# Branch C's local attention ahead of its states, branch D's token shift on GpSimd, and 12 instead of 14 early gate tiles

## The chip, the core and the metric

One core of a Trainium2 chip runs one program. The time is that of the device in microseconds. The engines are TensorE (PE; its weight loads are PEld), VectorE (DVE), ScalarE (ACT), GpSimd (POOL) and SyncE (SP, which only issues transfers here). They run side by side and wait for one another on semaphores. SBUF is the memory on the core, PSUM the eight banks that TensorE writes.

## The reference, cut to what matters

Three blocks follow one another on 512 tokens of width 1024. Only the first is touched. It projects the tokens, runs four mixers A to D on slices of the projection, and merges them under gates:

```
ys = jnp.stack([ya, yb, yc, yd], axis=2)
gates = jax.nn.sigmoid(p["gate"].reshape(bsz, seq, N_BRANCHES, D_MODEL))
merged = jnp.sum(gates * jnp.einsum('bsnc,ncd->bsnd', ys, w_branch[l]), axis=2)
x = _layer_norm(DN_ALPHA * x + merged @ w_out[l], ln_g[l, 0], ln_b[l, 0])
```

Branch C works in chunks of 64 tokens. Its output is a masked product inside each chunk plus the product with the state before the chunk, and the state is a chain over the chunks:

```
att = jnp.where(causal, jnp.einsum('bnihd,bnjhd->bnhij', q_dec, k_inv), 0.0)
o_intra = jnp.einsum('bnhij,bnjhv->bnihv', att, vc)
def step(state, inp):
    d, u = inp
    return d[..., None] * state + u, state
o = o_intra + jnp.einsum('bnihd,bnhdv->bnihv', q_dec, before)
```

Branch D first mixes each token with the one before it, then goes through a long recurrence:

```
def _token_shift(z, mu):
    prev = jnp.pad(z, ((0, 0), (1, 0), (0, 0)))[:, :-1]
    return z + (prev - z) * mu
```

After the first block come a mixture of experts with 32 experts and two more layers, neither of which the change edits.

## The kernel before, in words

Activations lie feature-major: a tile is 128 features by 512 tokens in fp32, and `pj` holds the 21 projected tiles. The program is a row of stages. Each `stage` ends with a barrier of all engines, and inside it every engine has its own list of instructions in the order in which the code writes them. There is no planner: the order is the code's. Where a step of DVE reads what the step before wrote, `Order` adds a semaphore wait.

The first block's stages in order are the projection, the attention of branches A and B in one stage (`attention`, called by `mixers_ab`), two small products, branch C (`mixer_c`: decays, a transposition, chunks and states, then `head_norm`), branch D (`mixer_d`: token shift, low-rank products, exponents, a transposition, `delta_chunks`), and `merge`.

The weights of the projections are split into a high and a low half, and a product is three matmuls (lines 193 to 195). `merge` computes 32 gate tiles (8 blocks of 3 matmuls each) and 32 branch tiles (2 blocks of 3), multiplies and adds them. Weights come in chunks of 16 blocks, which ACT rounds (line 160) and POOL or DVE subtracts (line 167).

Some of the 32 gate tiles are computed earlier, one fp32 matmul per block (line 251), as filler between the small matmuls of the mixers. `EARLY_GATES` says which. `k.gates.fill(pe, n)` puts n blocks into TensorE's list, `copy` lets ACT bring a finished tile to SBUF (line 262), and `move` lets SP store it to memory and load the next weights. In `merge` ACT loads these tiles back (line 680) and takes their sigmoid.

Before, 112 blocks (14 tiles) are filled in: 32 in the attention, 16 in branch C's decays, 8 in `head_norm`, and 16, 16 and 24 in the first three stages of `mixer_d`. Branch D's token shift is a stage by itself: 21 DVE instructions (lines 1497 to 1499), 16 filler blocks on TensorE, a table load on ACT.

In the attention, a step handles two units. TensorE computes scores (L881), DVE adds the bias and finds the maximum (L983, from a PSUM bank and an SBUF strip for branch A), ACT takes the exponential (L937), DVE divides in SBUF (L989 and L990), TensorE transposes the result (L896), ACT copies it (L946) and TensorE multiplies it with the values (L910). POOL has nothing to do there.

In branch C's stage of chunks TensorE computes the state updates (L1399), the scores within the chunks (L1405), and then for each half of the output the product with the states (L1412) and the product inside the chunks (L1417) into one bank. DVE makes the states (L1430, L1431), then masks the scores (L1437), and copies the result (L1441).

## Time and profile before

| | us |
|---|---|
| median of 3 runs (lowest, highest) | 2757.49 (2756.34, 2758.59) |
| the profiled execution's own time | 2755.97 |
| its span from the first to the last instruction | 2754.2 |
| PE busy in the span | 2615.7 (95%) |
| DVE busy | 1072.6 (39%) |
| ACT busy | 779.2 (28%) |
| POOL busy | 887.9 (32%) |

How to read it: the span lies 1.8 us inside the profiled execution's time. An engine's busy time is the time with at least one of its instructions under way. A row of the timeline gives start, duration, engine, line, operation, output and inputs, and in brackets the idle time before it with what ended it. A row of the windows gives a stretch, its length, the busy time and the number of instructions of PE, PEld, DVE, ACT and POOL, then the granted clock of TensorE (1.00 is 2.4 GHz, 0.50 is 1.2 GHz), the busy share of the DMA engines and GB/s. An fp32 matmul appears as two records.

### The profile page before, as it was taken

How to read it: one execution, taken by the hardware profiler on the slowest of the kernel's cores; microseconds unless marked ns; L12 is line 12 of the kernel's file. 1: busy time of each engine (PE TensorE's matmuls, PEld its weight loads, DVE VectorE, ACT ScalarE, POOL GpSimd, SP SyncE). 2: the span in 40 equal slices, each digit the busy share in tenths (PEclk: the TensorE clock that was granted, in tenths of full speed). 3: DMA queues.
4: the chain of work that ended last, by engine and by line, in shares of the span. 5: the costliest groups of instructions: out<-in, count | busy, mean ns of one | idle time of the engine just before them, and what ended most of it. 6: DMA issues, size and time to landing. Idle time of an engine off the chain costs nothing. (4 is left out here: it accounts for less than half of the span.)

```text
span 2754.2 us, 30647 instructions
## 1 busy us (share of the span) xinstructions
PE 2615.7 (95%) x12344; PEld 1917.8 (70%) x12344; DVE 1072.6 (39%) x1785; ACT 779.2 (28%) x1117; POOL 887.9 (32%) x273
## 2 busy tenths in 40 slices
PE   8988789999889999899999999999999999999998
PEld 6764448788533335784888888888675888888886
DVE  4854345355231113367344411222276444411211
ACT  3023222332121112526322422322326222422311
POOL 4620000044123332230444444444320444444443
PEclk9999789899989999999999999999999999999999
DMA  4431110133469996222222222222240222222223
GB/s 166 155 120 60 46 65 1 46 115 107 199 245 389 392 391 264 86 101 27 92 94 106 92 92 97 102 92 103 104 105 15 95 95 104 92 92 98 101 92 122
DMA packets 84173, 341.56 MB, mean 124 GB/s; under 512 B 34390, under 2 KB 34774, under 8 KB 48448
## 3 DMA queue, kind: packets, MB, share of 16 engines
q1 hardware_dynamic: 64216, 316.28, 31.6%
q10 hardware_dynamic: 5992, 14.87, 1.6%
q0 software_dynamic: 13824, 8.44, 1.0%
q8 instruction: 99, 1.62, 0.2%
q14 instruction: 42, 0.34, 0.0%
HBM read 381.04 MB, written 29.79 MB: 149 GB/s over the span
## 5 line engine op out<-in xcount | busy, mean ns | idle before, releaser
L167 POOL TENSOR_TENSOR w_lo<-w_raw,w_hi 128x2048 fp32r<-128x2048 f32 x148 | 689.2, 4656 | 1541.2 <-ACT w_hi L160 1520.4
L193 PE MATMUL bank<-xh,w_hi 128*128 128x512 f32 x1752 | 697.3, 398 | 29.5 <-DVE w_lo L373 10.9
L194 PE MATMUL bank<-xl,w_hi 128*128 128x512 f32 x1752 | 687.0, 392 | 0.0
L195 PE MATMUL bank<-xh,w_lo 128*128 128x512 f32 x1752 | 686.8, 392 | 0.0
L193 PEld LDWEIGHTS bank<-xh,w_hi 128*128 128x128 f32 x1752 | 332.2, 190 | 112.9 <-issue 30.2
L160 ACT ACTIVATE w_hi<-w_raw 128x2048 fp32r<-128x2048 f32 x150 | 286.4, 1909 | 360.5 <-PE bank L193 338.7
L194 PEld LDWEIGHTS bank<-xl,w_hi 128*128 128x128 f32 x1752 | 332.0, 189 | 73.2 <-issue 5.0
L195 PEld LDWEIGHTS bank<-xh,w_lo 128*128 128x128 f32 x1752 | 331.9, 189 | 69.3
L193 PE MATMUL bank<-ha,w_hi 128*128 128x512 f32 x480 | 186.7, 389 | 0.0
L194 PE MATMUL bank<-hb,w_hi 128*128 128x512 f32 x480 | 186.7, 389 | 0.0
L195 PE MATMUL bank<-ha,w_lo 128*128 128x512 f32 x480 | 186.7, 389 | 0.0
L2992 DVE TENSOR_TENSOR yb<-bank,mats 128x512 f32<-128x512 f32 x64 | 44.3, 692 | 205.8 <-PE bank L195 205.8
L251 PE MATMUL bank<-res,w_raw 128*128 128x512 f32 x224 | 110.7, 649 | 1.9 <-PEq L293 1.9
L3028 DVE TENSOR_TENSOR yb<-yb,bank 128x512 f32<-128x512 f32 x44 | 30.2, 687 | 203.3 <-PE bank L195 203.3
L2958 ACT ACTIVATE yb<-yb 128x512 f32<-128x512 f32 x64 | 40.4, 632 | 241.4 <-DVE yb L2992 241.4
L193 PEld LDWEIGHTS bank<-ha,w_hi 128*128 128x128 f32 x480 | 90.1, 188 | 18.8
L195 PEld LDWEIGHTS bank<-ha,w_lo 128*128 128x128 f32 x480 | 90.1, 188 | 18.7
L194 PEld LDWEIGHTS bank<-hb,w_hi 128*128 128x128 f32 x480 | 90.1, 188 | 18.4
L2138 PE MATMUL bank<-ring,xt 128*64 128x512 f32 x392 | 96.1, 595 | 0.0
L3025 DVE TENSOR_TENSOR yb<-bank,mats 128x512 f32<-128x512 f32 x44 | 30.4, 692 | 156.7 <-PE bank L195 144.1
L251 PEld LDWEIGHTS bank<-res,w_raw 128*128 128x128 f32 x224 | 44.9, 206 | 60.4 <-issue 60.3
L2974 ACT ACTIVATE ha<-yb 128x512 fp32r<-128x512 f32 x44 | 27.8, 632 | 204.7 <-DVE yb L3028 204.7
(581 smaller groups left out, 3549.4 us busy)
## 6 DMA issues: line engine op xcount, KB each, us to landing
w_raw<-weights SPq DMA_DIRECT2D x189, 1024.0 KB, 4.8
ring<-weights SPq DMA_DIRECT2D x49, 1024.0 KB, 10.1
before_halves<-weights SPq DMA_DIRECT2D x18, 1024.0 KB
res<-weights SPq DMA_DIRECT2D x16, 1024.0 KB
distance_bias<-distance_bias_once ACTq DMA_DIRECT2D x8, 512.0 KB
na_bias<-grid_bias SPq DMA_DIRECT2D x16, 240.0 KB, 6.4
strips<-distance_bias SPq DMA_DIRECT2D x8, 448.0 KB, 3.8
early_gates<-gate_rows SPq DMA_DIRECT2D x14, 256.0 KB, 2.0
```

The costliest lines, as they stand in the source:

```text
L160: act.activation(self.hi[:, s, :], self.raw[:, s, :], ACT.Copy).then_inc(self.rounded, 1)
L167: engine.tensor_tensor(self.lo[:, s, :], self.raw[:, s, :], self.hi[:, s, :].bitcast(F32), ALU.subtract).then_inc(self.split, 1)
L193: self.released(pe.matmul(out, hi, moving[0], start=start, stop=False))
L194: pe.matmul(out, hi, moving[1], start=False, stop=False)
L195: return pe.matmul(out, lo, moving[0], start=False, stop=stop)
L251: mm = pe.matmul(self.k.bank[self.banks[j]][:, :], self.k.ws.raw[:, c % 2, 128 * (b % 16):128 * (b % 16) + 128], self.k.res[:, t, :], star ...
L2138: last = pe.matmul(out[side_rows[side], :], xt[:, b % 3, columns_of(t, side)], g[:, SEQ * (t % 4):SEQ * (t % 4) + SEQ], start=t == 0, stop ...
L2958: act.activation(sig[:, u % 3, :], sig[:, u % 3, :], ACT.Sigmoid).then_inc(sigmoid_ready, 1)
L2974: act.activation(fh[:, j, :], mid, ACT.Copy).then_inc(row_rounded, 1)
L2992: dve.tensor_tensor(sig[:, u % 3, :], k.bank[u % 4][:, :], k.rstd, ALU.mult).then_inc(gate_scaled, 1)
L3025: dve.tensor_tensor(silu[:, j % 2, :], ffn_bank(j, 0)[:, :], k.rstd, ALU.mult).then_inc(act_scaled, 1)
L3028: dve.tensor_tensor(mid, silu[:, j % 2, :], ffn_bank(j, 1)[:, :], ALU.mult).then_inc(lin_read, 1)
```

## The change

`EARLY_GATES` becomes shorter by one in sixteen, so 12 tiles are computed early and 20 in `merge`. The token shift's stage goes, with its 16 filler blocks. The shift itself becomes a function `shift` that GpSimd runs inside the attention's stage, as 28 instructions: a subtraction, one for the first column, a multiplication with `mu`, an addition. ACT's table load of that stage moves into `head_norm`, before the copy of the gate tile. In branch C's stage of chunks TensorE computes the scores first, then the updates, then the products inside the chunks into banks 4 and 5, which ACT copies to `yb`, and last the products with the states into banks 6 and 7, which DVE adds to `yb`.

```diff
-EARLY_GATES = (0, 2, 4, 7, 9, 11, 14)
+EARLY_GATES = (0, 2, 5, 8, 10, 13)
...
+        if shift:
+            @block.gpsimd
+            def _(pool):
+                shift(pool, Order(pool, pool_order))
...
             if gates:
+                act.preload_act_table_set("sigmoid_and_others")
                 gates.copy(act, 1)
...
+        def shift(pool, step):
+            for j, t in enumerate([T1["dr"], T1["dr"] + 1, T1["dk"], T1["dk"] + 1, T1["dv"], T1["dv"] + 1, T1["low"]]):
+                rows = slice(0, 96 if t == T1["low"] else 128)
+                z, sh, mu = pj[rows, t, :], moved[rows, :], k.par1[rows, P1["mu"] + j:P1["mu"] + j + 1]
+                step(pool.tensor_tensor(sh[:, 1:SEQ], z[:, 0:SEQ - 1], z[:, 1:SEQ], ALU.subtract))
+                step(pool.tensor_scalar(sh[:, 0:1], z[:, 0:1], -1.0, None, ALU.mult))
+                step(pool.tensor_scalar(sh, sh, mu, None, ALU.mult))
+                step(pool.tensor_tensor(z, sh, z, ALU.add))
...
+                for p in range(2):
+                    act.wait_ge(inner_ready, p + 1)
+                    act.activation(k.yb[:, 4 + p, :], k.bank[4 + p][:, :], ACT.Copy).then_inc(inner_copied, 1)
...
+                for h in range(4):
+                    pe.wait_ge(att_masked, h + 1)
+                    rows = slice(64 * (h % 2), 64 * (h % 2) + 64)
+                    for t in range(4):
+                        last = pe.matmul(k.bank[4 + h // 2][rows, 128 * t:128 * t + 128], cv[:, t, 64 * h:64 * h + 64],
+                                         att[:, h, t, :], start=True, stop=True)
+                    if h % 2:
+                        last.then_inc(inner_ready, 1)
                 pe.wait_ge(states_ready, 1)
-                pe.wait_ge(att_masked, 4)
...
+                for n in range(7):
+                    dve.wait_ge(update_ready, 4 if n < 4 else 8)
...
+                    y = k.yb[:, 4 + p, :]
+                    dve.wait_ge(inner_copied, p + 1)
                     dve.wait_ge(out_ready, p + 1)
-                    dve.tensor_copy(k.yb[:, 4 + p, :], k.bank[p][:, :]).then_inc(out_copied, 1)
+                    dve.tensor_tensor(y, y, k.bank[6 + p][:, :], ALU.add).then_inc(out_copied, 1)
...
-        with stage(k, "vector_order") as (block, order):
-            @block.tensor
-            def _(pe):
-                k.gates.fill(pe, 16)
...
-            @block.vector
-            def _(dve):
-                step = Order(dve, order)
-                for j, t in enumerate([R, R + 1, K_, K_ + 1, V, V + 1, T1["low"]]):
-                    z = pj[:, t, :]
-                    step(dve.tensor_tensor(sh[:, 1:SEQ], z[:, 0:SEQ - 1], z[:, 1:SEQ], ALU.subtract))
-                    step(dve.tensor_scalar(sh[:, 0:1], z[:, 0:1], -1.0, None, ALU.mult))
-                    step(dve.scalar_tensor_tensor(z, sh, p1("mu", j), z, ALU.mult, ALU.add))
```

TensorE's list in branch C's stage of chunks, before (`ki`, `qd` the scores' inputs, `kut`, `cv` the updates', `st` the states, `att` the masked scores):

```order
L1399 MATMUL bank<-cv,kut 128x256 x8
L1405 MATMUL bank<-qd,ki 128x128 x16
L1412 MATMUL bank<-qd,st 128x64 x8
L1417 MATMUL bank<-att,cv 64x128 x8
L1412 MATMUL bank<-qd,st 128x64 x8
L1417 MATMUL bank<-att,cv 64x128 x8
```

and the same place now:

```order
L1422 MATMUL bank<-qd,ki 128x128 x16
L1426 MATMUL bank<-cv,kut 128x256 x8
L1432 MATMUL bank<-att,cv 64x128 x16
L1439 MATMUL bank<-qd,st 128x64 x16
```

The matmuls are the same in number and shape. The scores moved to the front, and all products with the states to the end.

TensorE's list from `head_norm` to branch D's low-rank products, before (L251 are filler blocks):

```order
L1097 MATMUL bank<-hn_sq,consts 128x512 x2
L251 MATMUL bank<-res,w_raw 128x512 x8
L288 UNCONDITIONAL_BRANCH
L292 ISA
L1479 UNCONDITIONAL_BRANCH
L251 MATMUL bank<-res,w_raw 128x512 x16
L288 UNCONDITIONAL_BRANCH
L1515 UNCONDITIONAL_BRANCH
L1520 MATMUL bank<-tl,mats_5 128x512 x6
```

and now:

```order
L1103 MATMUL bank<-hn_sq,consts 128x512 x2
L251 MATMUL bank<-res,w_raw 128x512 x8
L288 UNCONDITIONAL_BRANCH
L292 ISA
L1514 UNCONDITIONAL_BRANCH
L1519 MATMUL bank<-tl,mats_5 128x512 x6
```

One stage with its 16 blocks is gone from between them, and the blocks don't come back in another stage of the mixers.

GpSimd's list in the attention's stage, where there was nothing between two barriers, begins now with this (`moved` is a new tile of 512 columns):

```order
L956 UNCONDITIONAL_BRANCH
L1290 TENSOR_TENSOR moved<-pj 128x511
L1291 ISA
L1291 TENSOR_SCALAR moved<-pj 128x1
L1292 TENSOR_SCALAR moved<-moved,par_3 128x512
L1293 TENSOR_TENSOR pj<-moved,pj 128x512
```

The last four computing rows repeat for seven tiles. The `ISA` row stands there once.

## Rows read from the trace of the kernel before

**Rows 1.** The page: span, and busy time of the engines.

```profile
span 2754.2 us, 30647 instructions
PE 2615.7 (95%) x12344; PEld 1917.8 (70%) x12344; DVE 1072.6 (39%) x1785; ACT 779.2 (28%) x1117; POOL 887.9 (32%) x273
```

**Rows 2.** Windows of the attention and of merge, columns as explained above.

```profile
176.00:256.00 80.00, 68.92 (x368) 35.25 (x368) 35.80 (x140) 34.20 (x104) 0.00 (x0) 0.94 0.24 86
...
560.00:600.00 40.00, 40.00 (x178) 33.15 (x177) 20.47 (x18) 13.28 (x15) 18.47 (x4) 1.00 0.35 112
```

**Rows 3.** Timeline of ACT around the token shift's stage.

```profile
322.28 0.60 ACT L262 ACTIVATE gate_rows<-bank 128x512 f32<-128x512 f32 x1 [3.72 <-PE bank L251]
324.15 1.28 ACT L1485 ACT_TABLE_LOAD   x1 [1.27 <-PEq L293]
...
341.79 0.63 ACT L1505 ACTIVATE tl<-pj 16x512 f32<-16x512 f32 x1 [1.30 <-ACTq L293]
```

**Rows 4.** Groups of instructions in the token shift's stage, 324 to 341.5 us.

```profile
L251 PE MATMUL bank<-res,w_raw 128*128 128x512 f32 x32 | 15.7, 652 | 1.9 <-PEq L293 1.9
...
L1497 DVE TENSOR_TENSOR pj<-pj 128x511 f32<-128x511 f32 x7 | 4.8, 691 | 3.3 <-PEq L293 3.1
```

**Rows 5.** Timeline of PE in branch C's stage of chunks.

```profile
283.20 3.79 PE L1399 MATMUL bank<-cv,kut 64*128 64x256 f32 x16 [1.46 <-PEq L293]
286.92 3.22 PE L1405 MATMUL bank<-qd,ki 32*128 32x128 f32 x32
296.59 3.64 PE L1412 MATMUL bank<-qd,st 128*128 128x64 f32 x16 [6.45 <-DVE att L1437]
300.16 2.88 PE L1417 MATMUL bank<-att,cv 128*64 128x128 f32 x16
```

**Rows 6.** Timeline of DVE in the same stage.

```profile
287.03 0.42 DVE L1430 TENSOR_TENSOR st<-bank,first_consts 128x256 f32<-128x256 f32 x1 [4.55 <-PE bank L1399]
...
293.96 2.48 DVE L1437 TENSOR_TENSOR att<-bank,first_consts 128x512 f32<-128x512 f32 x4
...
309.50 0.69 DVE L1441 COPY yb<-bank 128x512 f32<-128x512 f32 x1 [5.73 <-PE bank L1417]
```

**Rows 7.** Windows of 1 us in the same stage.

```profile
286.00:287.00 1.00, 1.00 (x7) 0.35 (x3) 0.00 (x0) 0.00 (x0) 0.00 (x0) 0.50 0.00 0
...
300.00:301.00 1.00, 1.00 (x6) 0.88 (x6) 0.00 (x0) 0.00 (x0) 0.00 (x0) 0.50 0.00 0
```

**Rows 8.** Timeline of ACT in merge: the rounding of two successive weight chunks.

```profile
571.10 1.92 ACT L160 ACTIVATE w_hi<-w_raw 128x2048 fp32r<-128x2048 f32 x1 [7.96 <-PE bank L193]
...
581.98 1.92 ACT L160 ACTIVATE w_hi<-w_raw 128x2048 fp32r<-128x2048 f32 x1 [7.47 <-PE bank L193]
```

**Rows 9.** Groups of POOL's instructions over the whole span.

```profile
L167 POOL TENSOR_TENSOR w_lo<-w_raw,w_hi 128x2048 fp32r<-128x2048 f32 x148 | 689.2, 4656 | 1541.2 <-ACT w_hi L160 1520.4 <-DVE hb L3015 12.3 <-DVE ml L759 8.6
...
L147 POOL TENSOR_TENSOR w_hi<-w_raw,w_zero 128x2048 fp32r<-128x2048 f32 x12 | 44.0, 3666 | 42.5 <-PE bank L193 40.2 <-PE bank L201 2.2
```

**Rows 10.** Timeline of POOL and DVE in the projection.

```profile
39.66 4.60 POOL L150 TENSOR_TENSOR w_lo<-w_raw,w_hi 128x2048 fp32r<-128x2048 f32 x1
...
42.44 1.98 DVE L1242 TENSOR_SCALAR yb<-yb 128x256 f32<-128x256 f32 x1
...
59.46 0.41 DVE L1242 TENSOR_SCALAR yb<-yb 128x384 f32<-128x384 f32 x1
```

**Rows 11.** Waits in the attention, 176 to 256 us: total, times, longest.

```profile
PEld bank L896 <- DVE att_p L990: 8.5, 4, 3.3
```

**Rows 12.** Timeline of DVE in the attention, one of the divisions.

```profile
191.33 0.42 DVE L990 TENSOR_SCALAR att_p<-att_p,att_s 128x384 f32<-128x384 f32 x1
```

**Rows 13.** Timeline of PE in the attention.

```profile
192.04 0.85 PE L896 MATMUL bank<-consts,att_p 128*128 128x128 f32 x6 [1.32 <-ACT yb L946]
...
229.47 4.54 PE L251 MATMUL bank<-res,w_raw 128*128 128x512 f32 x6
...
236.40 2.84 PE L251 MATMUL bank<-res,w_raw 128*128 128x512 f32 x6
```

More of the change, by code:

```diff
@@ L835, in root_programs, with attention @@
     return names, dict(tensor=tensor, scalar=scalar, scalar_end=scalar_end, vector=vector)
-def attention(k, units, outs, probt, strip_loads=(), gates=None, kept=None):
+def attention(k, units, outs, probt, strip_loads=(), gates=None, kept=None, shift=None):
     steps = len(units) // 2
@@ L1298, in mixers_ab @@
                               select=select[:, i - 1, 0:n] if b and i else None, rows=rows, cols=tiles[i]))
-        attention(k, units, [yb[:, p, :] for p in range(4)], yb[:, 4:8, :], strip_loads=loads, gates=k.gates)
+        attention(k, units, [yb[:, p, :] for p in range(4)], yb[:, 4:8, :], strip_loads=loads, gates=k.gates,
+                  shift=shift)
     small_products(k, [(yb[:, 2 + p, :], k.mats1[:, 256 + 128 * p:384 + 128 * p], yb[:, 2 + p, :], None)
@@ L1385, in mixer_c @@
         turn(k, [(kut[:, :, :], [ku[:, 128 * t:128 * t + 128] for t in range(4)])])
-        with stage(k, "att_ready", "att_masked", "update_ready", "silu_ready", "states_ready", "out_ready",
-                   "out_copied", "vector_order") as (block, att_ready, att_masked, update_ready, silu_ready,
-                                                     states_ready, out_ready, out_copied, order):
+        with stage(k, "att_ready", "att_masked", "update_ready", "silu_ready", "states_ready", "inner_ready",
+                   "inner_copied", "out_ready", "out_copied", "vector_order") as (
+                       block, att_ready, att_masked, update_ready, silu_ready, states_ready, inner_ready,
+                       inner_copied, out_ready, out_copied, order):
             @block.scalar
@@ L1393, in _ @@
                     act.activation(g, g, ACT.Silu).then_inc(silu_ready, 1)
+                for p in range(2):
+                    act.wait_ge(inner_ready, p + 1)
+                    act.activation(k.yb[:, 4 + p, :], k.bank[4 + p][:, :], ACT.Copy).then_inc(inner_copied, 1)
             @block.tensor
             def _(pe):
-                for n in range(8):
-                    rows = slice(64 * (n % 2), 64 * (n % 2) + 64)
-                    pe.matmul(k.bank[update_bank(n)][:, update_cols(n)], kut[rows, n // 2, :], cv[rows, n // 2, :],
-                              start=True, stop=True).then_inc(update_ready, 1)
                 for h in range(4):
@@ L1406, in _ @@
                     last.then_inc(att_ready, 1)
+                for n in range(8):
+                    rows = slice(64 * (n % 2), 64 * (n % 2) + 64)
+                    pe.matmul(k.bank[update_bank(n)][:, update_cols(n)], kut[rows, n // 2, :], cv[rows, n // 2, :],
+                              start=True, stop=True).then_inc(update_ready, 1)
+                for h in range(4):
[6 more added lines that the diff above has]
+                        last.then_inc(inner_ready, 1)
                 pe.wait_ge(states_ready, 1)
-                pe.wait_ge(att_masked, 4)
                 for p in range(2):
-                    out = k.bank[p]
                     for n in range(8):
-                        pe.matmul(out[:, 64 * n:64 * n + 64], st[:, n, 128 * p:128 * p + 128],
-                                  qd[:, 64 * n:64 * n + 64], start=n == 0, stop=False, skip_group_check=True)
-                    for h in (2 * p, 2 * p + 1):
-                        rows = slice(64 * (h % 2), 64 * (h % 2) + 64)
-                        for t in range(4):
-                            last = pe.matmul(out[rows, 128 * t:128 * t + 128], cv[:, t, 64 * h:64 * h + 64],
-                                             att[:, h, t, :], start=False, stop=(h % 2 == 1 and t == 3),
-                                             skip_group_check=True)
+                        last = pe.matmul(k.bank[6 + p][:, 64 * n:64 * n + 64], st[:, n, 128 * p:128 * p + 128],
+                                         qd[:, 64 * n:64 * n + 64], start=True, stop=True)
                     last.then_inc(out_ready, 1)
```

27 lines of the change are left out of this document (9 added, 18 removed).

## Prediction

> **What bounds the kernel now.** I read the page first. TensorE is busy for 2615.7 us of a span of 2754.2 us [rows 1], so at most 5% of the span is there to be had from waits, and a matmul that is added where TensorE never pauses is paid in full. Then I read the windows by stage. In merge TensorE is busy for 40.00 us of 40 at clock 1.00 [rows 2]. In the attention it is busy for 68.92 of 80 us, and POOL, with 0 instructions, does nothing at all there [rows 2]. The mixers are a chain of short stages with barriers, so each stage is to be read by itself: what ends last in it sets where the next one begins. The change touches four places, and I take them in the order in which they weigh.
>
> **The token shift's stage goes.** ACT's first instruction in it starts at 324.15 us, and its first in the next stage at 341.79 us, each 1.3 us behind the barrier [rows 3]. So the stage with its barrier is worth 341.79 - 324.15 = 17.64 us. Its length is that of the 16 filler blocks, 15.7 us in 32 records, while DVE's share is short, for its 7 subtractions take 4.8 us [rows 4]. The table load that stood in it takes 1.28 us. It now comes before the copy in `head_norm`, where ACT sits idle for 3.72 us until the filler ends [rows 3], so it costs nothing. The neighbour stages keep their work and follow on each other. The pause that TensorE makes between them is of the old kind, so I count no change in them. **-17.64 us.**
>
> **The 16 blocks come back in merge.** Two more late gate tiles are 16 blocks, which is one weight chunk. Merge takes one chunk from one rounding to the next, 581.98 - 571.10 = 10.88 us [rows 8], that is 48 matmuls of 0.227 us. TensorE has no idle time there [rows 2], so all of it is on the path. The new chunk's rounding (1.92 us) and subtraction (4.66 us) [rows 8, 9] need 6.6 us of a period of 10.88, so they stay hidden. I went through the new order of blocks to see whether ACT could come late to a rounding, because a sigmoid ahead of it waits for DVE. In the old order and in the new one no rounding has to wait behind such a sigmoid. **+10.88 us**, and with the removal above it leaves -6.8 us.
>
> **Branch C's stage of chunks.** Before, TensorE does updates for 3.79 us and scores for 3.22 us. DVE has the states made from 287.03 to 293.96 us and then masks for 2.48 us. TensorE waits 6.45 us, and then needs about 12.9 us, two times 3.64 and 2.88 [rows 5, 6]. The last copy ends at 310.19 us [rows 6]. Now step by step, with the same durations: scores from 283.20 to 286.4, updates to 290.2, of which the first four are done at 288.3. The masks follow the scores head by head and end at about 287.1. The chain of states starts at 288.3, lasts 6.9 us, and with the small copy ends at 295.4. Meanwhile TensorE does the products inside the chunks, 2 x 2.88 = 5.8 us, to 296.0. The states are ready by then. The products with the states take 2 x 3.64 = 7.3 us, to 303.3, and the last addition ends at 304.05. ACT's two copies (0.6 us each) lie under them. The gain is 310.19 - 304.05 = 6.1 us.
>
> The clock makes this smaller or larger. At 286 us, after the idle time at the barriers, TensorE is granted 0.50, the lower level, 1.2 GHz [rows 7]. The 32 score records took 3.22 us mostly behind that stretch, and now they stand in it. At half the rate all of them would take 3.2 us more, so the bound from below is a gain of 3 us. At the other end the products with the states ran at 0.50 [rows 7], for the stretch from 300 us lies in them. If the unbroken run ahead of them holds 1.00, they could need half, and the gain is 9.7 us. I take 5.0, nearer to the row, because it shows the cold clock at the place where the scores go. **-5.0 us.**
>
> **GpSimd beside the attention.** The instructions are 14 two-input ones of 512 columns, 7 multiplications of 512 columns and 7 of one column. The nearest rows are 4.66 us for 2048 columns with two inputs, so 1.16 us for a quarter, and 3.67 us, so 0.92 us, for a lighter one [rows 9]. That makes 14 x 1.16 + 7 x 0.92 = 22.7 us, and with the starts and 28 waits for its own semaphore 25 to 30 us. The stage lasts from 177 to 255 us, so the pass itself is hidden. It runs to about 205 us, and nobody reads the shifted tiles before branch D.
>
> It is not free for DVE. The multiplication in SBUF at 42.44 us took 1.98 us for 256 columns and ended 0.16 us behind the POOL instruction that had begun at 39.66 us, while the same line needs 0.41 us for 384 columns at 59.46 [rows 10]. So DVE was held until POOL's instruction ended. The attention's divisions are of that kind, 0.42 us for 384 columns [rows 12], and TensorE's transposes wait for them four times, 8.5 us in all [rows 11]. Between these places TensorE has filler to do and a held division is absorbed. At 192.04 us it already waits 1.32 us [rows 13], and two divisions stand ahead of it. Each can be held by up to 1.16 us, and so can the pair of the step before. I take 2.6 us for the four. At the next such place, 209 us, the pass has ended or is in its last instructions: 1.0 us. A longer pause has one more price. The six filler records behind the pause at 228 us took 4.54 us, against 2.84 us at the full clock [rows 13], so 1.7 us, and with the holds the pause at 190 us becomes as long as that one. Together 5.3 us. The bounds are 0 (all holds land in slack) and about 21 (below). **+5.3 us.**
>
> The Trainium skill ("SBUF — State Buffer", the section on the engine side's shared port) says that GpSimd and a DVE operation with two SBUF inputs or in a 2-port mode take one port pair exclusively for a whole instruction, and the other blocks fully. The held row above agrees with it. If the port were divided instead of locked, a division of 0.42 us could lose at most its own length, and the term would be near 1 us.
>
> **The sum.** -17.64 + 10.88 - 5.0 + 5.3 = -6.5 us. Against the profiled execution's 2755.97 us (span 2754.2) that is 2749.5. The median of the runs lies 1.5 us above that execution, so I forecast 2757.49 - 6.5 = **2751.0 us**, 0.24% faster. Two differing kernels of this length can be told apart from about 0.2%, 5.5 us.
>
> **The rivals.**
>
> First, the holds are absorbed. For it speaks that DVE is busy for only 35.8 of 80 us in the attention [rows 2], against it that the four waits of rows 11 lie right at divisions. Then the term is 0.5 us, branch C gives its full 6.1, and the sum is -17.64 + 10.88 - 6.1 + 0.5 = -12.4: 2745.1 us.
>
> Second, GpSimd's pass is longer than I think and still runs at 209 us, so that this place pays in full too: 2.4 us for two held divisions and 1.7 us for filler at the lower level, in place of 1.0. The term becomes 8.4, the sum -3.4: 2754.1 us. For it speaks that no row shows a POOL multiplication by a column, that DVE's locked instructions delay POOL in turn (16 divisions of about 0.4 us), and that 28 starts are only guessed. Against it, my sum has it end 4 us earlier.
>
> The Trainium skill ("GPSIMD Engine Reference", Instruction dispatch) says that the first call of freshly loaded code on GpSimd pays about 6 us. POOL's new list has one `ISA` row ahead of its first multiplication. By that page the pass would end 6 us later, beyond 209 us, which is this second rival. No row of the trace before shows such a gap.
>
> Third, slower. GpSimd's multiplication by a column is so slow, or DVE and GpSimd hand the port to and fro so badly, that the pass lasts over most of the stage. Then all four places of rows 11 pay, 4 x (2.4 + 1.7) = 16.4 us, and in branch B the bias step with both inputs in SBUF is held as well, two units at each of two places, 4 x 1.16 = 4.6 us. The term is 21, the sum -17.64 + 10.88 - 5.0 + 21 = +9.2: 2766.7 us. It decides from a term of 17.3 on (0.2% slower), and needs a multiplication of over 5 us in place of 0.92. Nothing in the rows speaks for it.
>
> Fourth, merge doesn't take the chunk at its plain price, because the new distribution of the early tiles leaves DVE or ACT behind at some branch tile. It would add 1 to 4 us, to about 2753. Against it speaks TensorE's unbroken run in merge at 20.5 us of DVE in 40 [rows 2].
>
> **How the numbers follow.** My forecast has 0.45, the absorbed holds 0.22, the longer pass 0.23, the slower case 0.05, merge's trouble 0.05. The likeliest case by itself ranges from 2748 to 2754, by branch C's bounds and a term of 3 to 8 in the attention. Over all cases I take 2743 to 2757. Faster than 2752.0: two thirds of the forecast's cases (0.30), all of the absorbed ones (0.22), a few of the others (0.05), 0.57. Slower by 0.2%: 0.06. Within: 0.37.
>
> **What would show it.** In the profile after, ACT's tanh (now line 1504 or so) should start some 1.3 us behind the end of `head_norm`'s copy, with the table load before that copy. Merge from the first rounding to its last product should be longer by 10.9 us, with TensorE still unbroken. In branch C's stage the last addition should come 20 to 22 us behind the stage's first matmul, where the last copy came 27 us behind it, and the states' chain should begin before 289 us by the old time. POOL should show 28 instructions from 177 us on that end before 210, and some DVE divisions in that stretch should last 1 us or more. The attention should be 3 to 8 us longer. I am wrong if the attention's stage keeps its length, if merge grows by much else than 10.9 us, or if branch C's stage gains under 3 us.

## The result, and the profile after

The changed kernel runs in **2742.49 us** (median of 5 runs, 2735.78 to 2747.47), the kernel before, run beside it, in 2757.49 us. The ratio is 0.9947 with a 95% interval of 0.9929 to 0.9965, so it is 15 us or 0.53% faster. A second set of 6 runs gave a median of 2742.66 us and a ratio of 0.9941 (0.9919 to 0.9963). I had forecast 2751.0 us with a range of 2743 to 2757. The direction was right, the gain more than twice as large as I said, and the time lies just outside the range. The profiled execution took 2742.49 us, and its span is 13.5 us shorter than before's. Page of the kernel after, the lines that answer to [rows 1]:

```profile
span 2740.7 us, 30667 instructions
PE 2605.7 (95%) x12360; PEld 1917.0 (70%) x12360; DVE 1069.0 (39%) x1764; ACT 780.9 (28%) x1118; POOL 921.7 (34%) x302
```

TensorE has 16 more instructions and is busy 10 us less, DVE has lost 21 instructions and POOL has 29 more. Half of the 10 us has a plain cause: the 16 blocks took 15.7 us as filler, one fp32 matmul each [rows 4], and take 10.88 us as three matmuls each in merge. The rest comes with no less work, and that already points at TensorE's clock.

To see where the 13.5 us went I took the start of TensorE's first matmul in each stage, and from stage to stage the difference. In brackets is the part of that time in which the granted clock was 0.50. "Again" is a second profile of the same kernel.

```
                            before       before again      after        after again
projection               177.04 (10.2)  177.39 (10.2)  179.09 (10.2)  182.09 (13.7)
first attention           79.16 (10.2)   79.12 (10.2)   80.35 (10.3)   80.32 (10.3)
branch B's products        3.82 ( 0.0)    3.82 ( 0.0)    5.07 ( 3.4)    5.08 ( 3.4)
branch C, decays          20.79 ( 6.8)   20.79 ( 6.8)   19.14 ( 3.8)   19.14 ( 3.8)
branch C, turn             2.40 ( 2.2)    2.54 ( 2.5)    2.54 ( 2.5)    2.55 ( 2.5)
branch C, chunks          28.52 (25.1)   28.51 (25.1)   20.47 (10.7)   20.47 (10.7)
head_norm (+ shift)       32.05 ( 8.2)   31.94 ( 8.0)   14.46 ( 3.7)   14.46 ( 3.7)
branch D, low rank        22.91 ( 9.3)   22.79 ( 9.1)   21.72 ( 6.5)   21.72 ( 6.5)
branch D, norms + turn    33.42 ( 3.0)   33.39 ( 3.0)   31.93 ( 0.0)   31.92 ( 0.0)
branch D, delta rule     127.31 (17.7)  127.29 (17.8)  127.67 (17.8)  127.69 (17.8)
merge                    197.80 ( 9.6)  197.78 ( 9.6)  208.46 ( 9.5)  208.46 ( 9.5)
the rest                2028.95 (66.7) 2027.52 (65.3) 2029.79 (71.5) 2029.62 (71.3)
```

The four touched places give +1.19 (attention), -8.05 (chunks), -17.59 (shift) and +10.66 (merge), -13.8 us together. All untouched stages add +0.3, made of larger pieces of both signs: +2.05 in the projection, -2.7 in branch D's stages ahead of the delta rule and +0.8 in the rest among them. Between the projection and the end of merge the stages of these two pairs repeat within 0.2 us, the parts of clock in them too. That looked as if a kernel had its own course of the clock. Experiments 11 and 12 correct this below.

The shift stage. ACT of the kernel after, answering to [rows 3]:

```profile
313.17 1.28 ACT L1126 ACT_TABLE_LOAD   x1
317.25 0.60 ACT L262 ACTIVATE gate_rows<-bank 128x512 f32<-128x512 f32 x1 [2.80 <-PE bank L251]
319.14 0.63 ACT L1504 ACTIVATE tl<-pj 16x512 f32<-16x512 f32 x1 [1.30 <-PEq L293]
```

The tanh starts 1.30 us behind the barrier, directly after `head_norm`. The table load lies in what had been a wait of 3.72 us for the filler, and 2.80 us of that wait is left, so it is hidden. Merge, ACT of the kernel after, answering to [rows 8]:

```profile
546.10 1.92 ACT L160 ACTIVATE w_hi<-w_raw 128x2048 fp32r<-128x2048 f32 x1 [7.47 <-PE bank L193]
...
556.98 1.92 ACT L160 ACTIVATE w_hi<-w_raw 128x2048 fp32r<-128x2048 f32 x1 [7.47 <-PE bank L193]
```

The period is 10.88 us again, and merge is longer by 10.66 us. Branch C's chunks, PE of the kernel after and one DVE row, answering to [rows 5, 6]:

```profile
286.20 5.10 PE L1422 MATMUL bank<-qd,ki 32*128 32x128 f32 x32 [1.46 <-PEq L293]
291.23 3.79 PE L1426 MATMUL bank<-cv,kut 64*128 64x256 f32 x16
294.94 3.48 PE L1432 MATMUL bank<-att,cv 128*64 128x128 f32 x32
300.46 3.79 PE L1439 MATMUL bank<-qd,st 128*128 128x64 f32 x32 [2.04 <-DVE e_tmp L1458]
```
```profile
293.38 0.42 DVE L1455 TENSOR_TENSOR st<-bank,first_consts 128x256 f32<-128x256 f32 x1 [1.35 <-PE bank L1426]
...
304.35 0.69 DVE L1463 TENSOR_TENSOR yb<-yb,bank 128x512 f32<-128x512 f32 x1 [1.10 <-PE bank L1439]
```

The scores took 5.10 us in place of 3.22, in the cold clock as feared. The sixteen products with states took 3.79 us in place of the 7.3 I had counted: they ran at 1.00. GpSimd in the attention, kernel after, the last tile's four instructions as a sample:

```profile
205.97 1.04 POOL L1290 TENSOR_TENSOR moved<-pj 96x511 f32<-96x511 f32 x1
207.10 0.22 POOL L1291 TENSOR_SCALAR moved<-pj 96x1 f32<-96x1 f32 x1
207.41 1.64 POOL L1292 TENSOR_SCALAR moved<-moved,par 96x512 f32<-96x512 f32 x1
209.14 1.27 POOL L1293 TENSOR_TENSOR pj<-moved,pj 96x512 f32<-96x512 f32 x1
```

The pass runs from 179.07 to 210.41 us, 31.3 us. The multiplication by a column, which I had put at 0.92 us, takes 1.64. DVE and PE at the attention's first pause, kernel after, answering to [rows 12, 13]:

```profile
191.61 1.09 DVE L996 TENSOR_SCALAR att_p<-att_p,att_s 128x384 f32<-128x384 f32 x1
192.81 1.01 DVE L996 TENSOR_SCALAR att_p<-att_p,att_s 128x384 f32<-128x384 f32 x1
```
```profile
192.86 0.52 PE L897 MATMUL bank<-consts,att_p 128*128 128x128 f32 x3 [1.32 <-ACT yb L947]
193.88 0.55 PE L897 MATMUL bank<-consts,att_p 128*128 128x128 f32 x3 [0.49 <-DVE att_p L996]
...
195.26 4.16 PE L251 MATMUL bank<-res,w_raw 128*128 128x512 f32 x6
...
212.57 0.84 PE L897 MATMUL bank<-consts,att_p 128*128 128x128 f32 x6 [1.32 <-ACT yb L947]
```

Both divisions are held, from 0.42 us to 1.09 and 1.01, but TensorE waits only 0.49 us more. The first division's hold lies under the 1.32 us that TensorE waits for ACT anyway, and half of the second division passes beside the first three transposes. Behind that pause the six filler records take 4.16 us in place of 2.84. At 212.57 us nothing has changed.

### The profile page after: what moved, and what is told of

It reads as the page before. It is cut to its first block and busy times, and to the rows that moved or that the text cites. A ratio compares the mean times of both kernels' runs of the same rounds, so it can differ in the third digit from the quotient of the medians.

```text
span 2740.7 us, 30667 instructions
## 1 busy us (share of the span) xinstructions
PE 2605.7 (95%) x12360; PEld 1917.0 (70%) x12360; DVE 1069.0 (39%) x1764; ACT 780.9 (28%) x1118; POOL 921.7 (34%) x302
## 3 DMA queue, kind: packets, MB, share of 16 engines
q0 software_dynamic: 13824, 8.44, 1.0%
## 5 line engine op out<-in xcount | busy, mean ns | idle before, releaser
L193 PE MATMUL bank<-xh,w_hi 128*128 128x512 f32 x1768 | 703.4, 398 | 30.4 <-DVE w_lo L373 10.9
L2991 DVE TENSOR_TENSOR yb<-bank,mats 128x512 f32<-128x512 f32 x64 | 44.3, 692 | 204.3 <-PE bank L195 204.3
L251 PE MATMUL bank<-res,w_raw 128*128 128x512 f32 x192 | 92.3, 633 | 0.0
L3024 DVE TENSOR_TENSOR yb<-bank,mats 128x512 f32<-128x512 f32 x44 | 30.4, 692 | 156.7 <-PE bank L195 144.1
L796 DVE TENSOR_TENSOR yb<-bank,mats 128x512 f32<-128x512 f32 x16 | 11.1, 692 | 188.9 <-PE bank L195 188.9
```

The costliest lines, as they stand in the source:

```text
L193: self.released(pe.matmul(out, hi, moving[0], start=start, stop=False))
L251: mm = pe.matmul(self.k.bank[self.banks[j]][:, :], self.k.ws.raw[:, c % 2, 128 * (b % 16):128 * (b % 16) + 128], self.k.res[:, t, :], star ...
L2991: dve.tensor_tensor(sig[:, u % 3, :], k.bank[u % 4][:, :], k.rstd, ALU.mult).then_inc(gate_scaled, 1)
L3024: dve.tensor_tensor(silu[:, j % 2, :], ffn_bank(j, 0)[:, :], k.rstd, ALU.mult).then_inc(act_scaled, 1)
```

## The experiments

**1 to 4, on one chip with 22 runs of the kernel before (median 2755.18 us, 2746.17 to 2761.61).** The first leaves GpSimd's pass out, so its output lacks branch D's token shift.

```diff
-                  shift=shift)
+                  shift=None)
```

> The changed kernel with GpSimd's pass over branch D's seven tiles left out (28 instructions), so branch D computes without its token shift; nothing else differs. It prices what GpSimd's pass costs the first attention. Theory A (the prediction's term of +5.3 us was too large, as the attention took 80.35 us after against 79.15 before): this kernel's attention is 79.2 us again and the whole is 0.5 to 2 us below the changed kernel, about 2741 us. Rival B (the pass does cost about 5 us, and a luckier run of the clock hid it in the changed kernel's one profile): the whole is 4 us or more below the changed kernel, about 2737 us, and the attention near 75 us. Under A the divisions take 0.42 us each again in the stretch from 179 to 210 us, and TensorE does not stand 1.3 and 0.5 us at 193 us.

Measured: 2742.15 us (7 runs, 2740.84 to 2745.92), ratio 0.9958 (0.9942 to 0.9973). Without GpSimd's 28 instructions the kernel is no faster, as far as intervals of some 4 us to either side can tell. The attention takes 79.57 us, 0.8 less than after. The chunk stage takes 3.3 us more (23.77) and merge 2.4 less (206.04), and in both the time at the low clock moved the same way. By time A holds, and the divisions are back at 0.42 us. The wait of 1.32 us at 192 us stays, which A had put down to the pass. But the attention here begins otherwise than in the kernel after. PE, this kernel:

```profile
177.46 4.54 PE L251 MATMUL bank<-res,w_raw 128*128 128x512 f32 x6
...
192.10 0.85 PE L897 MATMUL bank<-consts,att_p 128*128 128x128 f32 x6 [1.32 <-ACT yb L947]
...
193.46 2.84 PE L251 MATMUL bank<-res,w_raw 128*128 128x512 f32 x6
```

The first filler is at the low clock and the one behind the pause is not. In the kernel after it is the other way round.

The second is the kernel before with branch C's new order alone (core of the edit):

```diff
-                for n in range(8):        # updates
-                    pe.matmul(k.bank[update_bank(n)][:, update_cols(n)], kut[...], cv[...], ...)
                 for h in range(4):        # scores
...
+                for n in range(8):        # updates
+                for h in range(4):        # inner products, into banks 4 and 5
+                    pe.wait_ge(att_masked, h + 1)
                 pe.wait_ge(states_ready, 1)
```

> The kernel before with branch C's new order alone: the scores first, the inner products in banks of their own, the copies on ScalarE and the adds; the shift stage and its gate chunk stay. Theory A (the order is worth 8.1 us, as its stage took 19.78 us against 27.84 and ran its products at the granted clock 1.00): 2749.4 us, ratio 0.997, with the sixteen products with states at 3.5 us. Rival B (the order is worth the predicted 5.0 us, and the other 3 us were a clock that happened to be up): 2752.5 us, with those sixteen products near 5.8 us in this kernel. The stage's length in the profile tells: 19.8 us under A, 22.8 under B.

Measured: 2750.97 us (12 runs, 2745.06 to 2758.07), ratio 0.999 (0.9977 to 1.0003): 4 us by the medians, and the interval just includes no change. The stage takes 23.45 us, 5.07 less than before, by far nearer to B. PE, this kernel:

```profile
287.61 5.11 PE L1405 MATMUL bank<-qd,ki 32*128 32x128 f32 x32 [1.46 <-PEq L293]
292.65 3.35 PE L1409 MATMUL bank<-cv,kut 64*128 64x256 f32 x16
295.93 2.57 PE L1415 MATMUL bank<-att,cv 128*64 128x128 f32 x32
301.88 6.78 PE L1422 MATMUL bank<-qd,st 128*128 128x64 f32 x32 [3.38 <-DVE e_tmp L1441]
```

The same 32 records of products with states take 6.78 us here and 3.79 us in the kernel after. The two stages differ by the same 3.0 us.

The third is the changed kernel with branch C's old order, the edit above reversed.

> The changed kernel with branch C's old order: the shift on GpSimd beside the attention, 12 early gate tiles, no shift stage. Theory A: -17.6 us of the stage, +10.9 of the gate chunk in the merge, +1.2 in the attention, so 5.5 us below the kernel before, 2752 us; branch C's stage is 27.8 us again. Rival B (the pass costs the predicted 5.3 us): -1.5 us, 2756 us. Rival C (the 3 us that untouched stages lost in the changed kernel come with this part and not with chance): -8.5 us, 2749 us. If e2 and this one add up to the whole change's -15 us the parts do not meet; if they add up to less, one needs the other.

Measured: 2742.82 us (10 runs, 2740.1 to 2748.43), ratio 0.996 (0.9945 to 0.9975). That is 12.4 us below the median of before, more than C and twice A. In its profile, from the attention on, it is 10.9 us below before: attention +0.3, shift -17.7, merge +8.24 (206.04 us, with 3.1 us at the low clock against 9.6), the stage behind merge -1.2, the rest -0.5. The chunk stage is at 28.52 us, as in before. So in this profile the pass cost 0.3 us and not 5.3, and the gate chunk was partly paid for by the clock. PE at the attention's first pause, this kernel:

```profile
193.67 0.85 PE L897 MATMUL bank<-consts,att_p 128*128 128x128 f32 x6 [1.32 <-ACT yb L947]
...
195.04 2.84 PE L251 MATMUL bank<-res,w_raw 128*128 128x512 f32 x6
```

Here one division in front of the pause lasts 0.81 us, but all of it lies under the wait for ACT: the six transposes follow on each other, where the kernel after had a second wait of 0.49 us between them. The medians of experiments 2 and 3 lie 4.2 and 12.4 us below before, 16.6 together, against 15.0 and 13.7 for the whole change, so within the noise the two parts add up.

The fourth lets GpSimd do all its instructions twice:

```diff
+            for j in range(7):
+                step(pool.tensor_tensor(sh[:, 1:SEQ], z[:, 0:SEQ - 1], z[:, 1:SEQ], ALU.subtract))
+                step(pool.tensor_scalar(sh[:, 0:1], z[:, 0:1], -1.0, None, ALU.mult))
+                step(pool.tensor_scalar(sh, sh, mu, None, ALU.mult))
+                step(pool.tensor_tensor(sh, sh, z, ALU.add))
```

> The changed kernel with GpSimd's 28 instructions done a second time, into a buffer that nobody reads, so that GpSimd works from 179 us to some 241 us, beside all of the first attention but its last part. Theory A (the pass costs by the holds of VectorE's divisions in front of the two waits, about 1 us for each of them): the second boundary at 212 us is now also under the pass, so 1 to 2 us above the changed kernel, about 2744 us, and the wait at 212.57 grows from 1.32 us to 2 to 3. Rival B (the forecast's second rival, holds of 3 us for a boundary and a half-clock filler behind each): 3 us or more, 2745.5 to 2748. Rival C (the holds are all absorbed): the same as the changed kernel within 0.5 us.

Measured: 2741.56 us (6 runs, 2739.83 to 2742.92), ratio 0.9951 (0.9934 to 0.9969). Rival C holds for the whole time. POOL, DVE and PE, this kernel:

```profile
240.93 1.26 POOL L1298 TENSOR_TENSOR moved<-moved,pj 96x512 f32<-96x512 f32 x1
```
```profile
210.03 1.00 DVE L996 TENSOR_SCALAR att_p<-att_p,att_s 128x384 f32<-128x384 f32 x1
...
228.76 0.99 DVE L996 TENSOR_SCALAR att_p<-att_p,att_s 128x384 f32<-128x384 f32 x1
```
```profile
210.60 1.04 PE L897 MATMUL bank<-consts,att_p 128*128 128x128 f32 x6 [1.32 <-ACT yb L947]
...
229.91 0.97 PE L897 MATMUL bank<-consts,att_p 128*128 128x128 f32 x6 [2.47 <-ACT yb L947]
```

GpSimd works until 242 us, DVE is busy 39.35 us of the 66 us from 178 to 244, against 31.01 without the pass in experiment 1, and TensorE's pauses keep their lengths or grow by 0.4 us (2.47 against 2.05 in experiment 1). The attention takes 80.02 us.

**5 to 8, beside 15 runs of before.** The fifth and sixth are the two kernels again.

> The kernel before once more, for a second profile of it. Its 22 runs beside the first four experiments went from 2746.2 to 2761.6 us, 15 us apart, where those of the changed kernel's family stayed within 8. Theory A (what varies is where TensorE's granted clock falls to 0.50, and by that the price of the same instructions): the stages of this profile that differ from the first one's differ by their time at 0.50, and branch C's chunk stage, 28.5 us with 25.1 us of it at 0.50 in both profiles that had the old order so far, is again near 28.5. Rival B (the transfers that feed the first projection vary): the whole difference to the first profile lies ahead of 178 us.

> The changed kernel once more, for a second profile and more runs beside the same runs of the kernel before as the other experiments. Theory A (branch C's stage is worth 5 us by its order and 3 us more when the clock stays at 1.00 in it, which it did in two of the four profiles with the new order): a median of 2741 to 2744, and a stage length from c2 to head_norm of either 20.5 or 23.5 us. Rival B (the first five runs were lucky): a median above 2745.

Measured: 2754.70 us for the one run of before, and 2742.66 us for after (6 runs, 2728.19 to 2745.31). The chunk stage was 28.51 and 20.47 us again. For before theory A holds: its stages from the attention to merge repeat, and what differs is 1.5 us in the last layers, with 1.4 us less at the low clock. B does not hold, for ahead of 178 us the second profile is 0.35 us longer. For after A holds too, and the 2.8 us between its two spans lie in the projection (179.09 against 182.09).

The seventh has 12 gate tiles in the kernel before, with the shift still a stage of DVE and no products in it.

```diff
-EARLY_GATES = (0, 2, 4, 7, 9, 11, 14)
+EARLY_GATES = (0, 2, 5, 8, 10, 13)
...
-                k.gates.fill(pe, 16)
...
-                k.gates.copy(act, 2)
...
-                k.gates.move(sp, 2)
```

> The kernel before with 12 early gate tiles instead of 14 alone: the shift stays a stage of VectorE, without gate products in it, and branch C's order is the old one. The gate chunk is then 10.9 us longer in the merge, and the shift stage shorter by what its products ran on after VectorE, 4 to 5 us. Theory A: +6 to +7 us to the kernel before, ratio 1.0024. Rival B (what the chunk costs in the merge is given back by the clock, whose time at 0.50 was shorter in the merge of two experiments that had the chunk there, 4.3 and 3.1 us against 9.6): +2 to +4 us.

Measured: 2763.32 us (10 runs, 2753.95 to 2766.78), ratio 1.0031 (1.0017 to 1.0045), +7.0 us by the medians. Theory A. ACT, this kernel, around the shift stage:

```profile
317.81 1.28 ACT L1481 ACT_TABLE_LOAD   x1 [1.27 <-PEq L293]
330.58 0.63 ACT L1496 ACTIVATE tl<-pj 16x512 f32<-16x512 f32 x1 [11.49 <-PEq L293]
```

The stage is 12.77 us with DVE's work alone, against 17.64 with the filler. So 4.9 us of the removal come from taking the products out and 12.8 from taking DVE's 21 instructions and the barrier out. Its profiled execution was its fastest run, at 2753.95 us, and shows about half of the 15 us over which before varies: attention 77.56 us in place of 79.16, branch C's decays 17.44 in place of 20.79, chunks 25.80 in place of 28.52, though in these stages it is the kernel before.

The eighth takes two more tiles out of the changed kernel, at the two places where filler ran on behind DVE:

```diff
-EARLY_GATES = (0, 2, 5, 8, 10, 13)
+EARLY_GATES = (0, 3, 6, 9, 12)
...
-                k.gates.fill(pe, 16)      # branch C's decays
+                k.gates.fill(pe, 8)
...
-                k.gates.fill(pe, 24)      # branch D's norms
+                k.gates.fill(pe, 16)
```

> The changed kernel with 10 early gate tiles instead of 12: one tile less in the stage of branch C's decays (eight products of 0.855 us) and one less in the stage of branch D's decays. In the changed kernel's profile TensorE's gate products end at 281.2 us in the first, 5.8 us after VectorE's last instruction, and 7.7 us after VectorE in the second. Theory A: -5.8 and -6.8 us there, +10.9 in the merge for one more chunk, so 1.7 us below the changed kernel, 2740 to 2741. Rival B (the products keep the clock up, and without them the stages behind run at 0.50): 2 us or more above the changed kernel. Rival C (the merge pays its 10.9 us in full but the two stages save less, since VectorE and ScalarE were the bound in them): +1 to +3 us, told from B by the clock in the stages behind.

Measured: **2739.19 us** (6 runs, 2737.29 to 2740.82), ratio to before 0.994 (0.9925 to 0.9956). The median is 3.5 us below that of after beside it, but the intervals of the two ratios overlap. Theory A by its total, not by its terms: decays -7.15 us where it had 5.8, norms -5.26 where it had 6.8, and merge +8.44 where it had 10.9, with only 3.3 us at the low clock. The other stages up to merge took 1.6 us more, most of it in the low-rank stage, whose time at the low clock rose from 6.5 to 9.5 us.

**9 to 12, beside 10 runs of before (median 2754.8 us).** The ninth puts the inner products back behind the states:

```diff
-                for h in range(4):
-                    pe.wait_ge(att_masked, h + 1)
...
+                pe.wait_ge(att_masked, 4)
                 pe.wait_ge(states_ready, 1)
                 for p in range(2):
                     for n in range(8):
...
+                    for h in (2 * p, 2 * p + 1):
```

> The changed kernel with branch C's inner products put behind the states again (each half's eight behind its products with states), while the scores stay in front of the updates. It tells which half of the new order is worth what. Theory A (the stage gains since the sixteen inner products run while VectorE still makes the states): the stage is longer by their 3.5 us and by the ScalarE copy behind them, 24 us at the higher clock, and the whole 3 to 4 us above the changed kernel. Rival B (the gain comes from the clock, which the late burst loses anyway): the products with states run at 0.50 again and the stage takes 27 to 28 us. Rival C (the stage's end is set by VectorE alone): within 1 us of 20.5.

Measured: 2747.39 us (6 runs, 2742.7 to 2750.07), ratio 0.9968 (0.9956 to 0.998), 4.7 us above after's second median (7.4 us below the runs of before beside it, where after was 13.7 below). The stage takes 27.70 us. PE, this kernel:

```profile
298.86 3.65 PE L1432 MATMUL bank<-qd,st 128*128 128x64 f32 x16 [5.83 <-DVE e_tmp L1457]
302.43 2.88 PE L1438 MATMUL bank<-att,cv 128*64 128x128 f32 x16
305.25 2.46 PE L1432 MATMUL bank<-qd,st 128*128 128x64 f32 x16
307.64 1.58 PE L1438 MATMUL bank<-att,cv 128*64 128x128 f32 x16
```

TensorE stands 5.83 us and then begins at the low clock, 3.65 and 2.88 us for records that take 2.46 and 1.58 a few microseconds later. That is B. Against the old order's 28.52 us, this kernel, with the scores in front of the updates, gains only 0.8 us, so in these profiles the inner products in the wait give the rest.

The tenth goes on to eight tiles, with half the filler in the attention.

```diff
-                    gates.fill(pe, (3, 3, 2, 0)[s % 4])
+                    gates.fill(pe, (2, 1, 1, 0)[s % 4])
```

> The kernel with ten gate tiles, with two of the four tiles of the first attention taken out too: eight early tiles, and one chunk more in the merge. Sixteen products of 0.47 us at full clock (six records, three products, took 2.84 us, so 0.95 a product of 512 columns in two passes) leave the attention, 15 us of TensorE's time, against 10.9 us in the merge. Theory A (in the attention TensorE is the bound between the boundaries): -8 to -13 us there, so 1 us below to 3 us above the kernel with ten tiles, 2738 to 2742. Rival B (without those products the attention waits on ScalarE and VectorE and the clock falls): -5 us or less there, 2745 us or more.

Measured: 2744.26 us (5 runs, 2743.15 to 2747.26), ratio 0.9962 (0.9949 to 0.9976). The attention is 10.15 us shorter than with ten tiles, as A has it, but the whole is above A's 2742: 10.5 us below the runs of before beside it, where ten tiles were 17.1 below. Merge takes 230.15 us against 216.90, 13.25 more, for its start is at the low clock for 9.4 us again in place of 3.3. Between kernels with equal time at the low clock in merge, a chunk costs 10.9 us each time (206.04 to 216.90; 208.46 to 230.15 for two).

> The kernel before with branch C's new order, for a second profile. Theory A (from the first attention on a kernel's stages repeat to within some tenths of a microsecond from run to run, as before and the changed kernel did): 23.4 to 23.5 us for branch C's stage again. Rival B (the clock falls anywhere): 20.5 as in the changed kernel.

> The changed kernel with branch C's old order, for a second profile. Theory A: the stages from the first attention on repeat, the merge at 206.0 us with 3.1 us of it at 0.50, and the attention at 79.5 us. Rival B: the merge is 208.5 us, as in both profiles of the changed kernel.

Measured, in this order: 2749.31 and 2745.15 us, one run each. Neither repeats its attention (77.57 and 80.37 us for 79.50 and 79.47) or its chunk stage: 20.43 us where the first profile had 23.45, and 26.11 where it had 28.52. So theory A is wrong as I had put it, while merge, at 197.76 and 206.06 us, repeats. A part of it shows at the attention's start. PE, experiment 11 (no pass), then experiment 12 (with the pass):

```profile
180.64 2.84 PE L251 MATMUL bank<-res,w_raw 128*128 128x512 f32 x6
...
195.38 2.84 PE L251 MATMUL bank<-res,w_raw 128*128 128x512 f32 x6
```
```profile
178.62 2.84 PE L251 MATMUL bank<-res,w_raw 128*128 128x512 f32 x6
...
192.99 0.55 PE L897 MATMUL bank<-consts,att_p 128*128 128x128 f32 x3 [0.36 <-DVE att_p L996]
...
194.37 4.18 PE L251 MATMUL bank<-res,w_raw 128*128 128x512 f32 x6
```

In both, the attention's first filler runs at the full clock, 2.84 us, where before and experiments 1, 3, 4 and 9 had it at the low one, 4.4 to 4.5 us. Without the pass the filler behind the pause stays at 2.84 us, and with the pass, after a pause 0.36 us longer, it takes 4.18. Thirteen profiles sorted by the first filler (us; experiment 10 left out, as its attention is another):

```
                        first filler at the low clock        first filler at the full clock
attention, no pass      79.16, 79.12, 79.57                  77.56, 77.57, 79.50
attention, with pass    79.47, 79.59; twice the pass 80.02   80.35, 80.32, 80.34, 80.37
chunks, old order       28.52, 28.51, 28.52                  25.80, 26.11
chunks, new order       23.77, 20.47                         23.45, 20.43, 20.47, 20.47, 20.46
```

In the left column the pass costs at most 0.5 us (79.47 and 79.59 against 79.12 to 79.57). In its three profiles with the pass no hold lengthens TensorE's pause: the wait is 1.32 us and the six transposes behind it take 0.85 or 0.86 us, as without the pass. In the right one it costs 2.8 us against the two profiles that keep the full clock up to 230 us, and 0.85 against the third, experiment 2, whose clock is low for 6.8 us there and not for 3.4. The chunk stage has a long and a short form in either order. Long against long the order is worth 28.52 - 23.45 = 5.1 us (4.8 with experiment 1's 23.77), short against short 25.80 - 20.43 = 5.4 to 26.11 - 20.47 = 5.6. The first filler sorts the forms of the old order, but not those of the new one. Which form a run takes is not in the kernel's text, for experiments 2 and 11, and 3 and 12, are each the same kernel.

## Why the prediction was wrong

By the profiled executions, forecast against measured: -17.64 and -17.59 for the stage, +10.88 and +10.66 for merge, -5.0 and -8.05 for branch C, +5.3 and +1.19 for the attention, 0 and +0.3 for all else. The miss of 7.0 us is two terms, the attention (4.1) and branch C (3.05). The medians are 1.5 us further apart than the executions.

**The step that failed most: "I take 2.6 us for the four", 1.0 at 209 us and 1.7 of filler.** In the kernel after each link of the mechanism is there. Divisions last 1.0 to 1.1 us, TensorE's pause grows, and the filler behind it falls to the low clock, 4.16 us in place of 2.84. The size was wrong. I let the holds of four divisions reach TensorE, and 0.49 us did. The pair of the step before was covered by filler, and at the pause itself TensorE waited for ACT's copy first. Rows 11 had misled me: they count what the weight loads waited for, while the matmul that I quoted from [rows 13] waited for ACT. The second pause, with held divisions in front of it in experiment 4, kept its wait of 1.32 us, and its transposes took 0.2 us longer. The Trainium skill ("SBUF — State Buffer", section "SBUF: two separate sides") has a whole-instruction lock on the port pair that DVE and GpSimd share, and the held divisions agree: they last longer than twice their 0.42 us. I had used that rule's price without the slack. My first rival, 2745.1 us with 0.5 for this term, was the nearest and had a chance of only 0.22.

The filler term of 1.7 has one more side. Where the first filler ran at the full clock, the pass cost up to 2.8 us: 0.49 of hold, 1.32 of filler, 0.5 in the matmuls around the pause and 0.5 later in the stage. Where the first filler ran at the low clock, the pause was not lengthened, the filler behind it stayed at the full clock, and the pass cost at most 0.5 us. The rows of before were of this second kind (4.42 us in its first filler). My sum took the hold and the fall from an attention that, in this form, has neither. A likely reason is the time of meeting: with the slow first filler TensorE's transposes start 15.0 us into the stage and not 13.8, while GpSimd's pass starts with the stage, so it meets other divisions. That is read from the profiles, and no run shifted the pass to test it. So the +1.19 us between the two first profiles mixes the forms: 1.6 us of what I gained there on my forecast is the first filler at the full clock (2.84 us in place of 4.42), which is luck and not a smaller hold.

**Branch C.** Form against form the order is worth 4.8 to 5.6 us, and I had said 5.0. That pairing is my reading: no run held the clock fixed. My steps were not right one by one: the products inside the chunks took 3.48 us and not 5.8, and TensorE then waited 2.04 us for the states, which I had ready by then. The remainder was in my text as the upper bound of 9.7 us ("if the unbroken run ahead of them holds 1.00"), and that is what the row of 3.79 us in place of 7.3 shows. I chose the value for the cold clock, and both profiles of the changed kernel have the short form, which the old order has too, in 2 of 5 profiles and worth 2.4 to 2.7 us there. So up to 3 of the 8 us are not the order's own. The new order was short in 5 of the 7 profiles above, so it may make the short form likelier, but seven are too few to say so.

**How the runs split the miss.** The terms above come from one pair of profiles. By the medians of many runs the order alone gave 4.2 us (experiment 2), near my 5.0, though its interval still includes no change. The kernel with the shift's part alone gave 12.4 us (experiment 3), where my terms for it say 1.5. So by the runs the larger part of the miss is not branch C. The attention's term explains 4 to 5 us of these 11, merge's time at the low clock 2.6 in that kernel's profile, and the rest stays open.

**"I count no change in them."** The neighbours did change: branch D's stages are 2.7 us shorter, the stage that begins with the router's matmuls 2.5 longer, and in each the time at the low clock moved the same way. Here it cancelled to 0.3 us. In experiment 3 it did not, and together with 0.3 us for the pass this gave -10.9 where terms read from rows had said -1.5.

**Right.** The stage's 17.64 us, the hidden table load and merge's plain price, and nearly the pass's length (25 to 30 us forecast, 31.3 measured, with longer multiplications). I had called DVE's share of the shift stage short, which experiment 7's 12.77 us contradicts, but the term did not rest on it. Of the signs that I had named, 3 to 8 us more in the attention did not come (1.19 us). The second rival's condition, a pass that still runs at 209 us, came true, but its price did not. For the sentence from the Trainium skill that stood beside it ("GPSIMD Engine Reference", section "Instruction dispatch", about 6 us for the first call of freshly loaded code) this trace shows no such gap: POOL's first instruction begins with TensorE's first in the stage, and its second 0.1 us behind the first.

```profile
179.07 1.04 POOL L1290 TENSOR_TENSOR moved<-pj 128x511 f32<-128x511 f32 x1 [18.85 <-POOLq L293]
180.21 0.23 POOL L1291 TENSOR_SCALAR moved<-pj 128x1 f32<-128x1 f32 x1
```

**What stays open.** What decides the form of a run's attention and chunk stage. Why merge begins with 9.5 us at the low clock in some kernels and with 3 in others, which is worth 2.4 us. How much of the 15 us is the change and how much a likelier form: of the 37 runs of before beside experiments 1 to 8, ten were at 2746.2 to 2749.2 us with a mean granted clock of 0.973 or 0.974, the others at 2751.7 to 2761.6 with 0.968 to 0.972, and both profiles of before belong to the latter. And why two runs of after were at 2728.19 and 2735.78 us, since no profile fell on one of them.

## What to carry to other kernels

A held instruction costs only what exceeds the wait that stands beside it, so take the pause's own releaser first. Where TensorE's clock moves, a stage's price is known only to within a clock fall: before an edit is credited with more than its matmuls and waits explain, look for the same stage with and without the edit at the same granted clock. Filler that outlasts the engine it covers is no cover: two gate tiles taken from such places made their stages 12.4 us shorter, more than the 10.9 us of their chunk in merge, but 1.6 us came back in other stages and the whole gain of 3.5 us is not clear of the noise.

## What the runs showed of the hardware that I had not expected

- GpSimd's multiplication of 512 columns by a per-partition column takes 1.57 to 1.64 us, more than its subtraction of two tensors of 511 columns (1.04 us) or their sum (1.27 us).
- Against no GpSimd work beside the attention, 56 instructions of it raised DVE's busy time from 31.01 to 39.35 us of 66, and the whole kernel's time not at all (2741.56 against 2742.15 us).
- The same 32 products took 6.78 and 3.79 us in two kernels with the same order in that stage, 3.0 us from TensorE's clock alone.
- The kernel before, unchanged, ran between 2746.2 and 2761.6 us, and the same program's chunk stage took 23.45 or 20.43 us (experiments 2 and 11). One profile shows one course of the granted clock, not the kernel's only one.
